# The activation rows of the expert dot products read from PSUM banks 4 to 7, with queries and key scores on banks 0 to 3

## The reference, cut to what matters

```python
def one_block(hb):                       # 128 tokens
    q = (hb @ w_q).reshape(PEER_BLOCK, PEER_HEADS, 2, PEER_HALF)
    sc = jnp.einsum('thcd,hcnd->thcn', q, sub_keys).astype(jnp.float32)
    s1, i1 = lax.top_k(sc[:, :, 0], PEER_TOPK)
    s2, i2 = lax.top_k(sc[:, :, 1], PEER_TOPK)
    ...
    top_s, pos = lax.top_k(cand_s, PEER_TOPK)
    idx = jnp.take_along_axis(cand_i, pos, axis=-1)
    g = jax.nn.softmax(top_s, axis=-1)
    u = u_tab[idx]
    act = jax.nn.gelu(jnp.einsum('thkd,td->thk', u, hb))
    wts = (g * act.astype(jnp.float32)).astype(hb.dtype)
    v = v_tab[idx]
    return jnp.einsum('thk,thkd->td', wts, v)
```

## Time and profile before

| | us |
|---|---|
| median of 3 runs | 2532.51 |
| lowest and highest of them | 2529.66, 2547.18 |
| the profiled execution, its own time | 2546.51 |
| its span in the profile | 2544.5 |
| from its first gather (492.0) to the last matmul on gathered rows (1276.2) | 784.2 |

### The profile page before, as it was taken

The page is one execution under the profiler, slowest core; times in us unless marked ns, Lnnn a source line. Parts: engine busy times, 40 slices in busy tenths (PEclk is TensorE's granted clock), DMA queues, the critical chain, the costliest instruction groups (busy, mean ns, idle before and its releaser), DMA issues.

```text
span 2544.5 us, 27270 instructions
## 1 busy us (share of the span) xinstructions
PE 2110.4 (83%) x8874; PEld 1185.0 (47%) x8875; DVE 1007.0 (40%) x2276; ACT 529.7 (21%) x945; POOL 555.5 (22%) x560
## 2 busy tenths in 40 slices
PE   7698798966655766666779987999999999999997
PEld 6566687832222322222367865444444444444443
DVE  5885511465665665665428423111111111111113
ACT  3414410121111111111122402222222222222221
POOL 0000000267776777677400000000000000000000
PEclk9898899988877877878889997999999999999999
DMA  6275253299898999899933242799999999999995
GB/s 281 100 292 204 108 206 117 77 362 380 304 360 334 365 359 375 326 362 344 403 115 133 100 165 99 305 380 429 429 428 429 429 429 429 429 429 429 429 428 231
DMA packets 111250, 784.27 MB, mean 308 GB/s; under 512 B 12993, under 2 KB 13249, under 8 KB 79585
## 3 DMA queue, kind: packets, MB, share of 16 engines
q1 hardware_dynamic: 37472, 515.18, 49.0%
q0 software_dynamic: 73728, 268.47, 28.2%
HBM read 782.55 MB, written 1.05 MB: 308 GB/s over the span
## 4 chain that ended last, share of the span: by engine, by line
PE 49%; issue 7%; DVE 2%; DMA 2%; POOL 1%; ACT 1%; POOLq 0%; another core or an unknown queue 0%; DVEq 0%; ACTq 0%
PE ps L661 41%; PE ps L810 6%; PE ps L1021 1%; DMA ring<-in_peer_v,arena 1%; DMA ring<-in_peer_u,arena 1%; POOL ring L615 1%; ACT arena L1203 1%; POOL ring L623 0%; PE ps L1052 0%; DVE arena L1647 0%; DVE arena L1650 0%; PE ps L1053 0%; DVE arena L1645 0%; PE ps L978 0%; DVE ring L1898 0%
## 5 line engine op out<-in xcount | busy, mean ns | idle before, releaser
L661 PE MATMUL ps<-ring,arena 128*64 128x512 f32 (+2 forms) x3328 | 743.1, 588 | 41.4 <-issue 40.0
L810 PE MATMUL ps<-ring,arena 128*128 128x512 f32 x1024 | 498.5, 645 | 247.0 <-issue 113.8
L661 PE MATMUL ps<-arena,ring 128*128 128x256 f32 x2272 | 521.1, 388 | 28.2 <-DVEq L1652 8.2
L661 PEld LDWEIGHTS ps<-ring,arena 128*64 128x64 f32 (+1 forms) x3328 | 259.7, 139 | 500.7 <-issue 499.4
L661 PEld LDWEIGHTS ps<-arena,ring 128*128 128x128 f32 x2272 | 438.4, 195 | 107.7 <-issue 38.1
L810 PEld LDWEIGHTS ps<-ring,arena 128*128 128x128 f32 x1024 | 209.4, 207 | 533.2 <-issue 528.2
L1630 DVE CUSTOM_DVE_ANT_0 ring<-ring,arena 128x1024 f32<-128x1024 f32 x256 | 312.4, 1226 | 172.7 <-DMA ring<-in_peer_u,arena 145.9
L615 POOL DMA_INDIRECT ring<-in_peer_u,arena x256 | 282.8, 1105 | 105.9 <-issue 80.4
L1871 DVE TENSOR_TENSOR arena<-ps,arena 128x512 f32<-128x512 f32 x66 | 45.7, 692 | 651.9 <-PE ps L1021 651.9
L661 PE MATMUL ps<-arena 128*128 128x128 f32 (+5 forms) x1494 | 232.9, 315 | 82.2 <-ACT arena L1122 20.3
L623 POOL DMA_INDIRECT ring<-in_peer_v,arena x256 | 256.6, 1003 | 102.8 <-issue 75.3
(11 more groups left out here) (292 smaller groups left out, 1073.9 us busy)
## 6 DMA issues: line engine op xcount, KB each, us to landing
ring<-in_w_exp SPq DMA_DIRECT2D x192, 2048.0 KB, 17.1
ring<-in_w_in SPq DMA_DIRECT2D x24, 2048.0 KB, 8.7
ring<-in_w_ada SPq DMA_DIRECT2D x12, 2048.0 KB, 9.4
ring<-in_w_out SPq DMA_DIRECT2D x4, 2048.0 KB, 8.2
ring<-in_w_peer_q SPq DMA_DIRECT2D x4, 2048.0 KB, 7.8
ring<-in_w_br_rnn SPq DMA_DIRECT2D x4, 1280.0 KB, 5.4
ring<-in_w_br_attn SPq DMA_DIRECT2D x2, 2048.0 KB, 8.1
ring<-in_peer_u,arena POOLq DMA_INDIRECT x256
```

The lines of the kernel that those rows point to most:

```text
L661: return pe.matmul(o, l, r, start=start, stop=stop)
L810: return pe.matmul(o, l, r, start=start, stop=False, skip_group_check=True)
```

## The change

`h2_rows` is no longer an SBUF tile filled by copies: it is a view of PSUM banks 4 and 5 (tile 0) and 6 and 7 (tile 1), where TensorE's transposes leave the rows. They stay there while a tile's dots read them as their second input, and VectorE frees the banks after a tile's loop. ScalarE's four copies and the semaphore `s_h2r` go. For this the list of jobs gives each job a bank of its own choosing (`banks_first`): `pq` and `key` jobs rotate over banks 0 to 3, `h2r` jobs have banks 4 to 7, all others keep the rotation over 8. The `h2r` jobs move from ahead of all `pq` jobs to behind the 2nd, 3rd and 4th pair of `pq` jobs and to the very end. `x2_rows`, the sums that ScalarE copies out after a tile, keeps the SBUF place. Lines below the change shift by 7 to 12.

```diff
-    s += [("h2r", i) for i in range(4)]
 
     for i in range(PH // 2):
         s.append(("pq", 2 * i))
         if i >= 1:
             s += [("key", i - 1), ("key", i + 3)]
         s.append(("pq", 2 * i + 1))
-    s += [("key", 3), ("key", 7)]
+        if i >= 1:
+            s += [("h2r", i - 1)]
+    s += [("key", 3), ("key", 7), ("h2r", 3)]
     return s
...
+def banks_first(plan):
+
+    narrow = ("pq", "key")
+    wide = [job for job in plan if job[0] not in narrow + ("h2r",)]
+    at = {job: n % N_BANKS for n, job in enumerate(wide)}
+    at.update({job: n % 4 for n, job in enumerate([job for job in plan if job[0] in narrow])})
+    at.update({("h2r", i): 4 + i for i in range(2 * TT)})
+    return [at[job] for job in plan]
...
-        h2_rows = carve("P", TT, D)
+        x2_rows = carve("P", TT, D)
+        h2_rows = [ps[:, 4 + 2 * t:6 + 2 * t, :].rearrange("p a b -> p (a b)") for t in range(TT)]
...
-            A.all_free(pe)
+            A.all_free(pe, range(4))
...
-                elif kind == "h2r":
-                    A.filled(act, *job)
-                    own(act.copy(h2_rows[:, i // 2, (i % 2) * 512:(i % 2 + 1) * 512], bank))
-                    act.sem_inc(free[b], 1)
-                    act.sem_inc(s_h2r, 1)
...
-                dve.wait_ge(s_h2r, 2 * (tile + 1))
+                A.filled(dve, "h2r", 2 * tile)
+                A.filled(dve, "h2r", 2 * tile + 1)
...
-                            dve.tensor_tensor_reduce(u_rows[k % 8], u_rows[k % 8], h2_rows[:, tile, :], 1.0, 0.0,
+                            dve.tensor_tensor_reduce(u_rows[k % 8], u_rows[k % 8], h2_rows[tile], 1.0, 0.0,
                                                      ALU.mult, ALU.add, dots[:, par, k:k + 1]).then_inc(s_dot, 1)
...
                 own.leave(PH // 2)
+                for half in range(2):
+                    dve.sem_inc(free[4 + 2 * tile + half], 1)
```

More of the change, by code:

```diff
@@ L173, with __init__, all_free @@
 class Jobs:
-    def __init__(self, plan, full, free, before=None):
-        self.number = {step: n for n, step in enumerate(plan)}
+    def __init__(self, plan, banks, full, free, earlier=None):
         self.full, self.free = full, free
-        self.base = [before.base[b] + before.jobs(b) if before else 0 for b in range(N_BANKS)]
-    def jobs(self, b):
-        return sum(n % N_BANKS == b for n in self.number.values())
+        self.base = [earlier.base[b] + earlier.uses[b] if earlier else 0 for b in range(N_BANKS)]
+        self.uses = [0] * N_BANKS
+        self.place = {}
+        for job, b in zip(plan, banks):
+            self.place[job] = (b, self.base[b] + self.uses[b])
+            self.uses[b] += 1
     def bank(self, *job):
-        return self.number[job] % N_BANKS
+        return self.place[job][0]
     def claim(self, pe, *job):
-        n = self.number[job]
-        if n >= N_BANKS:
-            pe.wait_ge(self.free[n % N_BANKS], self.base[n % N_BANKS] + n // N_BANKS)
+        b, uses = self.place[job]
+        if uses:
+            pe.wait_ge(self.free[b], uses)
     def filled(self, eng, *job):
[L194 to L199, removed]
+        b, uses = self.place[job]
+        return eng.wait_ge(self.full[b], uses + 1)
+    def all_free(self, eng, banks=range(N_BANKS)):
+        for b in banks:
+            eng.wait_ge(self.free[b], self.base[b] + self.uses[b])
 class Own:
@@ L422, in build_program @@
         s_v, s_a, s_p = sem("vector_own"), sem("scalar_own"), sem("pool_own")
-        A = Jobs(plan_first(), full, free)
-        B = Jobs(plan_second(), full, free, before=A)
+        A = Jobs(plan_first(), banks_first(plan_first()), full, free)
+        B = Jobs(plan_second(), itertools.cycle(range(N_BANKS)), full, free, earlier=A)
         def unit(name, i):
@@ L690, in _ @@
                     if first % 4 == 2:
-                        pe.wait_ge(full[b], A.number[job] // N_BANKS + 1).then_inc(unit_used("w_in", u), 1)
+                        A.filled(pe, *job).then_inc(unit_used("w_in", u), 1)
                 elif kind == "v":
@@ L759, in _ @@
                     project(A, job, b, w, 1, rnnT, CR, 1).then_inc(full[b], 1)
[L760 removed]
+                    A.filled(pe, *job).then_inc(unit_used("w_br_rnn", i), 1)
                 elif kind in ("bra", "wo"):
@@ L789, in _ @@
                     if i % 2 == 1:
-                        pe.wait_ge(full[b], A.number[job] // N_BANKS + 1).then_inc(unit_used("w_peer_q", i // 2), 1)
+                        A.filled(pe, *job).then_inc(unit_used("w_peer_q", i // 2), 1)
                 elif kind == "key":
@@ L803, in _ @@
                     if i == 7:
-                        pe.wait_ge(full[b], A.number[job] // N_BANKS + 1).then_inc(unit_used("sub_keys", 0), 1)
+                        A.filled(pe, *job).then_inc(unit_used("sub_keys", 0), 1)
                 else:
@@ L840, in release @@
                 def release(name, u):
-                    pe.wait_ge(full[b], B.base[b] + B.number[job] // N_BANKS + 1).then_inc(unit_used(name, u), 1)
+                    B.filled(pe, *job).then_inc(unit_used(name, u), 1)
                 if kind == "x2T":
@@ L1483, in _ @@
                     dve.wait_ge(s_root, 2)
-                    dve.wait_ge(full[A.bank("gate", 7)], A.number[("gate", 7)] // N_BANKS + 1)
+                    A.filled(dve, "gate", 7)
                     norm_h(lambda c: col("norm2_g", c))
```

9 lines of the change are left out of this document (4 added, 5 removed).

## The result

| | before | after |
|---|---|---|
| median of 4 runs each, side by side, us | 2536.03 | 2575.64 |
| ratio, 95% interval | | 1.013 (1.010 to 1.016) |
| span of the profiled execution, us | 2544.5 | 2572.9 |
| first gather, and length of the stage (first gather's start to last one's end), us | 492.0; 761.1 | 489.0; 791.1 |
| from the last gather to the end, us | 1291.4 | 1292.8 |

What follows compares the result with a forecast made beforehand. POOL's sequence of gathers was taken as the path through the retrieval stage. Holds of 53.3 us less 3.0, 4.0 and 3.0 gave 43.3, plus 1.4 for order: 44.7 off 2532.5, so 2488 us; range 2472 to 2516.

Steps and rivals of the forecast that it cites:

- Part 1, the holds: Retrieval stage: dots with two SBUF inputs hold POOL's gathers; a second input in PSUM removes 53.3 us of holds.
- B: Rival: dots hold POOL's gathers even with PSUM, because of how they run; 2531 us, chance 0.07.
- C: Rival: memory bounds the retrieval stage at 352 GB/s, so freeing POOL gives nothing; 2531 us, chance 0.04.
- Part 3, the dot: VectorE's dots: one input in PSUM changes a dot's time by 0; from above, 1 to 2 us in all.
- D: Rival: dots with PSUM run at half rate, near 2.3 us, and VectorE becomes the bound; 2589 us, chance 0.04.
- The fourth group ... This stays: Part 2: VectorE's unexplained spells of 9.67, 4.74 and 4.79 us within `best_keys`, and POOL's 7.04 us buffer wait, remain.
- DMA ... I take 3 us for it: Part 2: DMA engines just keep up, with a fuller queue, so rows land a bit later; -3.0 us.
- first group: Part 2: the first group's `u` holds are hidden, since its `v` gathers wait for the last keys; -3.0 us.
- Part 2, the route: Faster `v` gathers only lengthen POOL's route wait in three to four of eight odd groups; -4.0 us.
- Part 4: New order and banks: transposes leave the first query's way; first `v` gathers come 1.4 us sooner, no wait added.
- Rival A: Half is taken back: full DMA lengthens route waits and VectorE's spells; gain 20 to 34 us, 2505, chance 0.17.

Runs made afterwards that it cites:

- r5: The changed kernel as it stands, run again on chip 13: 2450.9 us against 2490.5 for the kernel before, ratio 0.985.
- e1: The changed kernel with its new order, but rows copied to SBUF again and read there by the dots: 2536.1 us, 0.998 of the kernel before.
- r6: The changed kernel with only tile 0's dots reading PSUM, tile 1's reading an SBUF copy, on chip 13: 2470.4 us, 0.992 of the kernel before.
- the written-out kernel: The changed kernel with VectorE's loop over pairs of heads written out, on chip 6: 2453.6 us, 0.986 of the kernel before.

## Why the prediction was wrong

By its own steps:

- **Part 1, the holds.** Right. 53.3 us of holds were to go; the gathers' means fell by 165 and 55 ns, 56 us. Rivals B (hold stays) and C (memory bounds: chip 13 moves 402 GB/s over the whole stage) fall. The Trainium skill's rule of the shared port pair (SBUF — State Buffer, "Who interferes with whom") holds for this kind of dot: 1.99 us down to 0.94.
- **Part 3, the dot.** Right: 1219 ns, 1226 before. The 65 ns more for PSUM, worked out in the prediction from the Trainium skill's figures (Perfetto Trace Analysis, "Optimizing Scalar/DVE Operations"), don't show in it. D named the right victim, VectorE, for a wrong reason.
- **Part 2, "The fourth group ... This stays", and "DMA ... I take 3 us for it".** This is the step that failed. I counted the spells of the earlier trace rows as an accident of one group whose cost stays as it is, and priced a fuller queue by when rows land. The rows landed about as before: by the packets, a `u` gather's last one ended 4.1 us (median) behind the gather's end before, 4.5 in the first result and 4.3 in r5. What grew were the spells: 112 to 256 us. The trace of before had it: only two of its groups ran at the full 41 to 43 us, the third (42.8 us from its first gather to the next group's) and the eleventh (42.0), and in the groups right behind these two the spells of 4.7 and 9.7 us stood, with 56.9 and 53.9 us. All others took 46 to 50 us with no more than one spell of 3 us or more. I read the spell as a cause of the slow group and didn't ask what had come ahead of it. I took 10 us off the 53.3 for everything that POOL would wait for in their place (first group, route, DMA); 86 us were to be taken off.
- **Part 2, the route.** "-4.0" for longer route waits: 27.9 us more were measured (10.1 to 38.0), for the same reason, since `route` comes behind the late dots of an odd group and has spells of its own.
- **Part 4.** The order gave what it was to give: first gather at 489.0, and e1 alone at 0.998. But the first `v` gather was to come at 515 and came at 524.9. TensorE's last but one lot of key matmuls had stalls of their own, with POOL at full pace beside them:

```profile
503.30 0.27 PE L673 MATMUL ps<-ring,arena 128*128 128x128 f32 x1 [0.67 <-issue]
506.11 0.27 PE L673 MATMUL ps<-ring,arena 128*128 128x128 f32 x1 [2.54 <-issue]
508.21 0.37 PE L673 MATMUL ps<-ring,arena 128*128 128x128 f32 x1 [1.83 <-issue]
510.31 0.37 PE L673 MATMUL ps<-ring,arena 128*128 128x128 f32 x1 [1.73 <-issue]
```

  On chip 13 the same matmuls are one piece of 1.95 us, and the first `v` gather starts at 515.35.
- **Rival A** came nearest (route waits and spells lengthen at the full pace), with a price that no row gave: at most 25 us taken back, where it was over 70. Its reason, full DMA engines, isn't enough: on chip 13 they are as full, without spells.

On chip 13 the forecast's reasoning holds with its size: 39.6 us gained in r5 (2490.5 to 2450.9) against 44.7 forecast, and r6 ascribes half of it to the holds of one tile. (On chip 6 only the written-out kernel ran, 35.7 us faster than before.) The kernel before takes 2532 to 2546 us on chips 12, 9 and 5, and the 2532.5 of the start are like those. So on a chip like those the prediction fails, and it said nothing of chips.

## What to carry to other kernels

An idle spell "for nothing that the profile names" is a price that depends on something: look at what the other engines did in the 20 us ahead of it, in every place where it stands, before you write "this stays". When an engine is set free, ask whether the pace that it reaches was ever held in the old trace, and what the waiting engines did just then; here two groups out of 16 had it and both were followed by the spells. A step that waits for its own short instructions is the one that suffers, so either keep such steps out of full-pace stretches or leave the fast engine a pause: one at every 4th gather bought back up to 43 us on chip 12, one at every 8th 12 us on chip 9 and cost some 33 us on chip 6. Where a change shifts the load by a few per cent, time it on more than one chip: one and the same kernel was 1.6% slower on one and 1.5% faster on another. And count whether a trace still holds its records before you read idle time from it.

## What the runs showed of the hardware

- Five chips, one batch on each, fell into two kinds: the kernel before at 2532 to 2546 us on three and at 2489 to 2491 us on two, the changed one at 2560 and 2571 on two of the three (2576 in the first result) and at 2451 on one of the two. The difference lies in the stretch with gathers (stage of the changed kernel 777 to 791 us against 663); from the last gather to the end all 18 runs take 1287 to 1300 us.
- A dot with two SBUF inputs lengthened a GpSimd gather that began just behind its start to 1.99 us; with the second input in PSUM a `u` gather takes 0.94 us, the longest 1.14.
- A dot product with one input in PSUM takes 1219 ns, with both in SBUF 1226.
- A semaphore increment of 21 ns took up to 1385 ns on VectorE on chip 5 and never over 21 on chip 13, with POOL's gathers freed on both.
- The traces of chips 12, 9 and 5 lack up to four fifths of the records of DMA landings in the stage (1570 to 3076 of some 8140 left), except with a pause at every gather (8005); those of chips 6 and 13 have all.
- A 128x1 memset of GpSimd with a wait for its own mark costs 0.61 us between two `v` gathers (1.85 us from gather to gather instead of 1.24) and 0.69 between two `u` gathers, though it is busy for 0.11 us.
